# Splitting the first weight load in two, and norming the queries' and feed-forward's input of one layer by halves of the tokens

## What is computed

```python
for layer in range(DEPTH):                       # DEPTH = 2
    xn = rms_norm(x, mix_norm[layer])
    if layer % 2 == 0: mixed = fox_diff_mixer(xn, ...)
    else:              mixed = mlstm_mixer(xn, ...)           # h, then h @ w_out
    x = x + mixed
    x = x + memory_cross_attention(rms_norm(x, xattn_norm[layer]), rms_norm(mem, mem_norm[layer]), wq, wkv, wo)
    x = x + conv_ffn(rms_norm(x, ffn_norm[layer]), w_up, conv_w, conv_b, w_down)
```

## Time and profile before

| | |
|---|---|
| median of 3 runs | 2633.13 us (2629.62 to 2634.3) |
| the profiled execution | 2635.62 us, span 2633.8 us |
| mean granted TensorE clock | 0.979 |
| TensorE matmul busy | 2559.1 us, 97% |
| VectorE, ScalarE, GpSimd busy | 1176.8, 528.5, 569.0 us |

### The profile page before, as it was taken

How to read it: one execution, slowest core, us unless ns; L and a number is a source line. 1 busy time by engine, 2 the same in 40 slices (tenths; PEclk the granted TensorE clock), 3 DMA queues, 4 the chain that set the end, 5 groups by cost and what they waited for, 6 DMA issues and landing times.

```text
span 2633.8 us, 35027 instructions
## 1 busy us (share of the span) xinstructions
PE 2559.1 (97%) x13350; PEld 2008.4 (76%) x13350; DVE 1176.8 (45%) x2379; ACT 528.5 (20%) x1149; POOL 569.0 (22%) x494
## 2 busy tenths in 40 slices
PE   8999999999899999999999999999999999999999
PEld 5857899986578998644567767888846864899997
DVE  3024178751413887314646763554400235434750
ACT  1131122111212220212530002222200123212220
POOL 0010135100112540001432321333200004332530
PEclk9989999999899999998999999999999997999999
DMA  6322255743234556210024571222211120243442
GB/s 236 128 96 94 98 216 183 258 174 144 80 128 160 183 220 224 77 72 25 1 77 146 209 271 65 73 87 96 114 50 76 71 107 1 97 154 150 164 180 104
DMA packets 39626, 335.20 MB, mean 127 GB/s; under 512 B 3792, under 2 KB 10064, under 8 KB 22352
## 3 DMA queue, kind: packets, MB, share of 16 engines
q1 hardware_dynamic: 39504, 333.50, 34.3%
HBM read 332.44 MB, written 1.05 MB: 127 GB/s over the span
## 4 chain that ended last, share of the span: by engine, by line
PE 86%; DVE 4%; DMA 4%; POOL 2%; issue 2%; ACT 1%; DVEq 0%; SPq 0%; POOLq 0%; ACTq 0%
PE PS L553 25%; PE PS L752 23%; PE PS L1474 6%; PE PS L1320 5%; PE PS L2407 5%; PE PS L1138 3%; PE PS L2448 3%; PE PS L1486 3%; DMA slot<-in_weights 3%; PE PS L1984 2%; PE PS L1149 2%; PE PS L1161 2%; PE PS L430 1%; PE PS L734 1%; PE PS L2100 1%
## 5 line engine op out<-in xcount | busy, mean ns | idle before, releaser
L553 PE MATMUL PS<-arena,slot 128*128 128x256 f32 x1696 | 372.3, 382 | 17.8 <-DMA slot<-in_weights 12.0
L553 PEld LDWEIGHTS PS<-arena,slot 128*128 128x128 f32 x1696 | 324.4, 192 | 63.6 <-issue 12.2
L553 PE MATMUL PS<-XN,slot 128*128 128x256 f32 (+1 forms) x1248 | 312.6, 411 | 5.0 <-DVE XN L492 5.0
L752 PE MATMUL PS<-SQ,slot 128*128 128x128 f32 (+1 forms) x1984 | 294.6, 301 | 3.8 <-DVE slot L848 3.8
L553 PEld LDWEIGHTS PS<-XN,slot 128*128 128x128 f32 x1248 | 238.0, 191 | 76.7 <-issue 42.5
L752 PEld LDWEIGHTS PS<-SQ,slot 128*128 128x128 f32 x1984 | 268.1, 191 | 17.3 <-DVE slot L848 4.3
L752 PE MATMUL PS<-XN,slot 128*128 128x128 f32 (+1 forms) x1664 | 250.0, 301 | 0.0
L752 PEld LDWEIGHTS PS<-XN,slot 128*128 128x128 f32 x1664 | 226.1, 192 | 10.7
L875 DVE SCALAR_TENSOR_TENSOR arena<-PS,small,arena 128x255 f32<-128x255 f32 (+2 forms) x352 | 174.7, 543 | 50.6 <-ACT arena L819 50.2
L819 ACT ACTIVATE arena<-PS,small 128x256 f32<-128x256 f32 (+1 forms) x176 | 105.2, 616 | 385.6 <-DVE PS L908 245.1
L1474 PE MATMUL PS<-arena,slot 128*128 128x512 f32 (+1 forms) x392 | 157.0, 562 | 3.2 <-POOL arena L2560 2.4
(11 more groups left out here) (245 smaller groups left out, 3468.8 us busy)
## 6 DMA issues: line engine op xcount, KB each, us to landing
slot<-in_weights SPq DMA_DIRECT2D x86, 2048.0 KB, 7.7
arena<-in_mod SPq DMA_DIRECT2D x96, 512.0 KB, 3.5
slot<-in_weights SPq DMA_DIRECT2D x16, 2816.0 KB, 9.7
slot<-in_weights SPq DMA_DIRECT2D x24, 1536.0 KB, 6.8
slot<-in_weights SPq DMA_DIRECT2D x2, 2176.0 KB, 8.9
slot<-in_weights SPq DMA_DIRECT2D x4, 1024.0 KB, 4.7
arena<-in_c SPq DMA_DIRECT2D x3, 1024.0 KB, 10.2
small<-in_small SPq DMA_DIRECT2D x1, 2685.0 KB, 19.1
```

The lines of the kernel that those rows point to most:

```text
L553: mm = pe.matmul(o, l, r, start=k == 0, stop=k == len(terms) - 1, skip_group_check=True)
L752: mm = pe.matmul(PS[:, bank, 0:h], lhs[:, k * P:(k + 1) * P], rhs(k), start=first and k == 0, stop=last and k == 3, skip_group_check=True)
```

## The change

Slab 0 is loaded by two DMAs of 1 MB with a semaphore each, and TensorE waits for the second only at tile 16. `add_out_halves` gains a form without a gate (a plain add) and takes the place of `add_out` and `add_norm` for `mixout1` with `xnorm1` and for `xo1` with `fnorm1`. The first four output tiles of `xq1` are computed by token halves (`tensor_first_halves`); the last four stay whole. The first up step of `a1` waits for the norm of each half by itself. `wo1` calls the same helpers, with no change in what it does. Layer 0 is unchanged.

```diff
@@ next_tiles
-            if t == 0:
+            if g == 0 and t == 0:
+                pe.wait_ge(sems["landed_first"], 16)
+            elif t == 0 or (g == 0 and t == 2 * DK):
                 pe.wait_ge(sems[f"landed{g % 2}"], 16 * (g // 2 + 1))
@@ add_out_halves
             def read(dve, m, g):
+                if gate is None:
+                    dve.tensor_tensor(X[:, m, part[g]], PS[:, m % 4, part[g]], X[:, m, part[g]], ALU.add)\
+                        .then_inc(*tick(VD, s, "read", m, g))
+                    return
@@
+        TOKEN_HALVES = [slice(0, P), slice(P, T)]
+        def half_norms(s, gain, before, shift=None):
+            return [[f"{s}{g}", norm_x(f"{s}{g}", X, XN, gain, after_out_half(before, g), [0], shift=shift, span=(g * P, P))]
+                    for g in range(2)]
+        def tensor_first_halves(pe, s, ready):
+            w = next_tiles(pe, 4 * DK)
+            for g in range(2):
+                for m in range(4):
+                    if g == 0 and m % 2 == 0:
+                        claim(pe, m // 2)
+                    c = TOKEN_HALVES[g]
+                    for k in range(DK):
+                        if m == 0:
+                            pe.wait_ge(*of(*ready(k, g)))
+                        a = (m * DK + k) * P
+                        mm = pe.matmul(PS[:, m // 2, (m % 2) * T:(m % 2 + 1) * T][:, c], w[:, a:a + P], XN[:, k, c],
+                                       start=k == 0, stop=k == DK - 1, skip_group_check=True)
+                    if g and m == 1:
+                        mm.then_inc(*tick(TD, s, "job", 0))
+                    elif g and m == 3:
+                        finish(mm, s, "job", 1)
+            for j in range(2):
+                lend(j, (s, "read", j, 0))
@@ layer 1
-                add_out("mixout1", lambda k: O1[:, k, :], lambda k: ("lstmgated", k // 2), DK, [0])
+                x_halves = half_norms("xnorm1", lambda m, g: col("xattn_norm1", m), "mixout1")
+                add_out_halves("mixout1", lambda k, c: O1[:, k, c], lambda k: [("lstmgated", k // 2)], DK, range(4, DK),
+                               None, x_halves, (0, DK - 1), TOKEN_HALVES)
@@
-                add_norm(s, units)
-            add_linear(f"xq{l}", ...)
+                def tensor_xq(pe, q_jobs=q_jobs):
+                    tensor_first_halves(pe, "xq1", lambda k, g: (f"xnorm1{g}", "out", 0, k))
+                    tensor_linear(pe, "xq1", q_jobs[2:], 2)
+                add(tensor=tensor_xq, scalar=lambda a, q_jobs=q_jobs: reads_linear(a, SD, "scalar", "xq1", q_jobs))
@@
-                add_norm(s, units)
+                f_halves = half_norms("fnorm1", lambda m, g: col("ffn_norm1", m), "xo1")
+                add_out_halves("xo1", lambda k, c: O1[:, k, c], lambda k: [("xatt1", "out", k // 2)], DK, range(4, DK),
+                               None, f_halves, (0, DK - 1), TOKEN_HALVES)
@@
-            add_ffn(f"a{l}", "a", [0], lambda m, g, s=s: [(s, "out", 0, m)], aside=(
+            add_ffn(f"a{l}", "a", [0], lambda m, g, l=l: [("fnorm0" if l == 0 else f"fnorm1{g}", "out", 0, m)], aside=(
@@ SP's program
-                load(g, len(table[g][1]), piece(g))
+                if g == 0:
+                    sp.dma_start(slots[0][:, 0:2 * DK * P], piece(0)[:, 0:2 * DK * P]).then_inc(sems["landed_first"], 16)
+                    sp.dma_start(slots[0][:, 2 * DK * P:4 * DK * P], piece(0)[:, 2 * DK * P:4 * DK * P])\
+                        .then_inc(sems["landed0"], 16)
+                else:
+                    load(g, len(table[g][1]), piece(g))
```

More of the change, by code:

```diff
@@ L267, in two_blocks @@
         for n in ("tensor_done", "scalar_done", "vector_done", "gpsimd_done",
-                  "landed0", "landed1", "mod_landed0", "mod_landed1", "mod_landed2", "mod_landed3", "late_landed0", "late_landed1", "loaded_c", "loaded_x", "loaded_mem", "loaded_ctx", "loaded_small", "loaded_rest",
+                  "landed0", "landed1", "mod_landed0", "mod_landed1", "mod_landed2", "mod_landed3", "late_landed0", "late_landed1", "loaded_c", "landed_first", "loaded_x", "loaded_mem", "loaded_ctx", "loaded_small", "loaded_rest",
                   "conv_done", "mod_done", "stored"):
@@ L1907, in two_blocks @@
                 add(gpsimd=gpsimd_gate)
-                add_out("mixout1", lambda k: O1[:, k, :], lambda k: ("lstmgated", k // 2), DK, [0])
+                x_halves = half_norms("xnorm1", lambda m, g: col("xattn_norm1", m), "mixout1")
+                add_out_halves("mixout1", lambda k, c: O1[:, k, c], lambda k: [("lstmgated", k // 2)], DK, range(4, DK),
+                               None, x_halves, (0, DK - 1), TOKEN_HALVES)
             s = f"xnorm{l}"
-            units = norm_x(s, X, XN, lambda m, g, l=l: col(f"xattn_norm{l}", m), after_out(f"mixout{l}", [0], None),
-                           [0])
+            q_jobs = feature_jobs(xn, at_out(s, DK), 8, lambda j, bank: [
+                ("scalar", act_op(Q1[:, 2 * j:2 * j + 2, :], copies(None, bank), scale=-0.0625))])
             if l == 0:
+                units = norm_x(s, X, XN, lambda m, g: col("xattn_norm0", m), after_out("mixout0", [0], None), [0])
                 add_norm_within(s, units, "memk0", memory_keys(0))
+                add_linear("xq0", q_jobs)
             else:
-                add_norm(s, units)
-            add_linear(f"xq{l}", feature_jobs(xn, at_out(s, DK), 8, lambda j, bank: [
-                ("scalar", act_op(Q1[:, 2 * j:2 * j + 2, :], copies(None, bank), scale=-0.0625))]))
+                def tensor_xq(pe, q_jobs=q_jobs):
+                    tensor_first_halves(pe, "xq1", lambda k, g: (f"xnorm1{g}", "out", 0, k))
+                    tensor_linear(pe, "xq1", q_jobs[2:], 2)
+                add(tensor=tensor_xq, scalar=lambda a, q_jobs=q_jobs: reads_linear(a, SD, "scalar", "xq1", q_jobs))
             add_attention(f"xatt{l}", cross_units(l), [(f"xq{l}", "read", 3, 0)] + (
@@ L1921, in two_blocks @@
                 [("memk3", "read", 0, 0), ("memv0", "tokread", 1), ("memv1", "tokread", 1)]))
-            add_out(f"xo{l}", lambda k: O1[:, k, :], lambda k, l=l: (f"xatt{l}", "out", k // 2), DK, [0])
             s = f"fnorm{l}"
-            units = norm_x(s, X, XN, lambda m, g, l=l: col(f"ffn_norm{l}", m), after_out(f"xo{l}", [0], None), [0])
             if l == 0:
+                add_out("xo0", lambda k: O1[:, k, :], lambda k: ("xatt0", "out", k // 2), DK, [0])
+                units = norm_x(s, X, XN, lambda m, g: col("ffn_norm0", m), after_out("xo0", [0], None), [0])
                 add_norm_within(s, units, "memk1", memory_keys(1))
             else:
-                add_norm(s, units)
+                f_halves = half_norms("fnorm1", lambda m, g: col("ffn_norm1", m), "xo1")
+                add_out_halves("xo1", lambda k, c: O1[:, k, c], lambda k: [("xatt1", "out", k // 2)], DK, range(4, DK),
+                               None, f_halves, (0, DK - 1), TOKEN_HALVES)
             ctx_norm = norm_x("bnorm_ctx", X, XN, lambda m, g: GAIN[:, 0, 0, m, g:g + 1], [[] for _ in range(4)], [1],
                               shift=lambda m, g: MOD[:, 0, m, g:g + 1])
-            add_ffn(f"a{l}", "a", [0], lambda m, g, s=s: [(s, "out", 0, m)], aside=(
+            add_ffn(f"a{l}", "a", [0], lambda m, g, l=l: [("fnorm0" if l == 0 else f"fnorm1{g}", "out", 0, m)], aside=(
                 "bnorm_ctx", ctx_norm, lambda a: (a.wait_ge(*of("modgain", 0, 0)), a.wait_ge(sems["loaded_ctx"], 16)))
@@ L2580, in two_blocks @@
             else:
[L2581 to L2584, removed]
+                norms = half_norms(s, lambda m, g, l=l: GAIN[:, l, 1, m, g:g + 1], f"wo{l}", mod_col(l, 3))
                 add_out_halves(f"wo{l}", lambda k, c: Y[:, k, c], lambda k, l=l: [(f"merge{l}", "merged", k)], DK,
-                               range(4, DK), gate1, norms, (0, DK - 1), part)
+                               range(4, DK), gate1, norms, (0, DK - 1), TOKEN_HALVES)
                 add_ffn(f"b{l}", "b", segs, lambda m, g, s=s: [(f"{s}{g}", "out", 0, m)], gate2)
```

## The result

| | before | after |
|---|---|---|
| median of 4 runs each | 2631.38 us (2629.53 to 2634.3) | 2614.64 us (2611.31 to 2617.4) |
| ratio | | 0.9935 (0.9918 to 0.9952) |
| profiled execution, span | 2635.62 us, 2633.8 us | 2614.83 us, 2613.0 us |
| mean granted TensorE clock | 0.979 | 0.984 |

The kernel is faster by 16.7 us in these runs. The forecast was 11.5 us, and the measured time lies 2.9 us under the low end of the range. Of the 7.0 us between the forecast of 2621.6 and the measured 2614.6, 5.2 us are gain beyond the forecast. The other 1.8 us are the kernel before itself: a fourth run moved its median from 2633.13 to 2631.38. The profiled executions differ by still more, 20.8 us of span, so the question is where the 9.3 us beyond the forecast come from in them.

A forecast was written before the change was run, and what follows sets the result against it. TensorE, busy for 97% of the span and 86% of the chain, was taken as the bound. Terms -2.5 - 4.7 - 4.3 = -11.5 us took the median from 2633.1 to 2621.6 us, range 2617.5 to 2626.

The forecast's parts named there:

- Term A: Start of the kernel: slab 0 in two halves lets TensorE start earlier, -2.5 us (from -2.2 to -2.8).
- Rival 1: First slab: its halves land together or each pays its own fixed cost; gain 0.5 us or less, time 2623.6; chance 0.12.
- Term B: mixout1, xnorm1 and xq1: less waiting and no slow clock, minus the price of half records, -4.7 us (-2.5 to -6.0).
- Rival 3: Half records in mixout1, xq1, xo1 run at the low clock; with half of them slow, 2643 us; chance 0.03.
- Rival 4: Norms' program order on VectorE holds the last reads back, TensorE still waits its 5 us; time 2628; chance 0.05.
- Term C: xo1, fnorm1 and up stage: first up step starts earlier, partly given back to in_c's load, -4.3 us (-3.0 to -5.2).
- I take a1's own time: Layer 1's up stage: in_c assumed to land 10.6 us after xo1's last slab ends, as in the kernel before.
- Rival 2: Feed-forward gives its share back, through in_c late by some 4 us or a1's early steps; time 2625.9; chance 0.08.
- From there to the end all stages should keep their lengths: Expected sign: after step 1 of layer 1's up stage, no later stage changes its length.
- about 2 us by which the shown runs differ: Allowance in the forecast range for differences among the shown runs of the kernel.
- Theory 1: Follow-up experiments: chance; the change gives its three terms, and the rest is how single executions differ.
- Theory 2: Follow-up experiments: shift; the change brings later stages into a better phase, so 16 to 17 us come every time.

The follow-up runs named there:

- this part alone: Only xo1 and fnorm1 by halves, up to the up stage, against the kernel before: 2627.29 us, ratio 0.9988.
- the quarter: The whole change with the first half of slab 0 split again into two transfers of 0.5 MB, wait at tile 8: 2616.64 us, ratio 0.9947 against the kernel before.
- the whole xq1: The whole change, but xq1 with whole tiles, waiting for both halves of the norm: 2625.14 us, ratio 0.9979 against the kernel before.

## Why the prediction was right and wrong

**The mechanism was right, and all three terms lie within their bounds.**

- *Term A*, -2.5 forecast: -2.4 measured (12.02 to 9.62). The half slab landed 0.06 us from its forecast. Rival 1 falls: the first half landed at 9.49 us, 2.4 before the whole slab did (11.89), so the halves neither land together nor pay about 2 us one after the other. The Trainium skill puts a fixed cost of about 2.0 us on a transfer of the GpSimd path ("DMA: Bandwidth & Descriptors", section "Anatomy of one DMA"); the 9.49 us of the trace show that in this queue it is not paid in series.
- *Term B*, -4.7 forecast: -5.0 measured. The 0.3 us are in the waiting (1.01 us before the second L432 where wo1 has 1.32); the slow clock gone and the price of half records came as forecast. Rival 3 (the low clock for half records) falls: the clock is 1.00 over xq1's first records, where it was 0.50 before. Rival 4 (edits without effect) falls by the same rows, though its mechanism is on the chain: VectorE's first-half norm does stand ahead of the last reads. It costs next to nothing, because the last tile's own square ends at 742.17, when GpSimd's held-back sum ends at 742.21.
- *Term C*, -4.3 forecast: -3.6 measured. The step that was off by 0.7 us is "I take a1's own time" for `in_c`: from the end of xo1's last slab (818.08) to the SiLU (829.43) it took 11.35 us, not 10.6. The rest of that chain, 5.02 us, was exact. In the run of this part alone the load took 10.35 us from issue to SiLU and the term came to -4.2; in the three profiles of the whole change and that of the quarter it took 10.8 to 11.0. Why the same loads take longer there is not shown. Rival 2 was right in kind and wrong in size: the feed-forward gives back 1.74 us, as the run with an earlier `in_c` shows, and not some 4. The prediction named the right wait.

By the rows the sum is -11.0, where -11.5 was forecast. Set against all the executions that were made, the change is worth 12 to 13 us, and their median of 2618.3 us lies within the range given, 3.3 us under the point: 2.2 us because the three runs that the forecast started from lie that far above the kernel's own median of 2630.9, and 1.1 us of gain.

**The step that failed is the last:** "From there to the end all stages should keep their lengths", together with the allowance of "about 2 us by which the shown runs differ". Stages without any edit had other lengths in the next execution. The attention stretch of the last layer took 21.2, 15.0, 17.8 and 21.2 us in the four profiles whose stretch rows stand above; over all twelve profiles of this study it lies between 15.0 and 21.3, in seven of them at 20.6 or more, with no order by kernel. Late slabs cost 1.1 to 1.6 us each, at a place that changes from profile to profile. Three shown runs, 4.7 us apart, were taken as if they showed the spread, and the profiled execution as if its later stages were the kernel's. Executions of one kernel in fact cover 14 us (2622.9 to 2636.9), with a standard deviation of 3.0. A median of four is then uncertain by some 3 us, and its difference to another median of four by some 5; below the forecast's 2621.6 the range had room for 4.1 us, against the 7.0 that were measured.

Theory 1 stands for most of it: the changed kernel itself, measured again, gave back some 4 of the 5.2 us by which the first 16.7 exceeded the forecast. Theory 2 falls in the size that the first pair suggested.

**What stays open.** Between the rows' 11.0 and the pooled 12 to 13 us are 1 to 2 us, about as much as the uncertainty. There is a candidate, of theory 2's kind. The four profiles without xo1's halves have three, two, one and one waits for late slabs in the up stages a1 and b1, 2.3 us on average; of the eight with xo1's halves seven have none and one, that of the whole xq1, has one of 1.13 us. (In the up stage a0, ahead of xo1, eleven of the twelve profiles have one each, whatever the kernel.) If that is not chance, the halves of xo1 spare about 2 us of late slabs. No run tested it.

## What to carry to other kernels

Where two stages are joined by a norm over features, split the tokens on both sides of it: the producer's last tiles by halves, so that the first norm starts early, and also the consumer's first tiles, so that the second norm is covered; the second of these keeps the clock up as well. When a stage is brought forward, look for the load that was covered by its delay and issue it earlier too. For changes below 0.5%, read the gain as a sum of local differences between fixed events of the two traces, and run the unchanged kernel again before any difference elsewhere is explained.

## What the runs showed of the hardware beyond that

- **A lightly loaded stretch costs another time in each execution.** 48 to 50 records of the last layer's attention take 13.3 us at a mean granted clock of 0.86, 16.1 at 0.70 and 19.5 at 0.56, with nothing changed in the program.
- **The slow start costs another time in each execution too.** The first 32 records take 9.10 to 9.87 us when begun between 9.5 and 9.9, 9.87 when begun at 8.58, 9.75 when begun at 9.20, and 8.55 to 9.6 when begun at about 12.1; at full clock 32 x 0.216 = 6.9 us would do. So a start that comes a microsecond earlier can't be priced from one profile.
- **VectorE and GpSimd hold each other up.** L864 took 1.64 us while GpSimd's L934 ran beside it, where the same operation took 0.69 in the kernel before, and L934 itself took 1.64 where it took 1.27 there. The Trainium skill says on "SBUF — State Buffer", section "SBUF: two separate sides", that the two share a port pair which one instruction holds to its end while the other blocks, for VectorE operations with two inputs in SBUF among others; the trace agrees. On this path it cost nothing, since ScalarE's chain was later.
